# Stationary blocks in chunk order for the first expert pair's one-hot products, and six zero products in the routing's waits

## The reference

```
g_sel  = top-1 of 4 expert groups (x @ w_group);  2 experts e of 8 in that group (x @ w_expert)
h      = silu(x[rows of e] @ w1[e]) * (x[rows of e] @ w3[e])
out   += (h @ w2[e]) * gate        # for each of the 32 experts e
```

## Time and profile before

| what | value |
|---|---|
| time, median of 3 runs | 1101.12 us (1099.44 to 1103.45) |
| the profiled execution: its time | 1100.17 us |
| its span, first to last instruction | 1098.3 us |
| mean granted TensorE clock | 0.992 of full |
| PE busy | 96% of the span |
| DVE, ACT, POOL busy | 37%, 25%, 9% |
| HBM traffic over the span | 266 GB/s; 412 GB/s in the long stretches of the experts |

### The profile page before, as it was taken

How to read it: one execution, slowest core, us unless ns; L and a number is a source line. 1 busy time by engine, 2 the same in 40 slices (tenths; PEclk the granted TensorE clock), 3 DMA queues, 4 the chain that set the end, 5 groups by cost and what they waited for, 6 DMA issues and landing times.

```text
span 1098.3 us, 12899 instructions
## 1 busy us (share of the span) xinstructions
PE 1053.3 (96%) x4563; PEld 543.0 (49%) x4597; DVE 401.2 (37%) x975; ACT 272.8 (25%) x530; POOL 99.7 (9%) x146
## 2 busy tenths in 40 slices
PE   6999999999999999999989999999999999999998
PEld 3577655333333334676655333333334844555543
DVE  1164424443443351462343443344430222333221
ACT  4244322111111003334321111111112005564300
POOL 1220221000000002210121000000000200000000
PEclk9899999999999999999999999999999999999999
DMA  8526227999999996427246999999979537822000
GB/s 299 195 78 256 103 87 246 386 412 411 412 413 412 411 399 208 128 82 302 77 172 228 398 412 413 412 412 412 413 289 389 199 36 201 310 85 77 1 1 38
DMA packets 95326, 280.44 MB, mean 255 GB/s; under 512 B 15957, under 2 KB 29699, under 8 KB 86960
## 3 DMA queue, kind: packets, MB, share of 16 engines
q1 hardware_dynamic: 90208, 273.27, 65.9%
q0 software_dynamic: 5072, 6.56, 1.7%
HBM read 286.98 MB, written 4.72 MB: 266 GB/s over the span
## 4 chain that ended last, share of the span: by engine, by line
PE 75%; SPq 14%; DMA 5%; issue 2%; ACT 2%; DVE 1%; ACTq 0%; DVEq 0%
PE bank L1464 12%; PE bank L922 12%; SPq L583 11%; PE bank L1029 8%; PE bank L954 6%; PE bank L1226 5%; PE bank L1043 5%; PE bank L873 4%; DMA ring<-in_w 3%; SPq L589 3%; PE bank L1610 3%; PE bank L1594 3%; PE bank L1482 3%; PE bank L862 2%; DMA ring<-in_w_in 2%
## 5 line engine op out<-in xcount | busy, mean ns | idle before, releaser
L922 PE MATMUL bank<-ring,arena 128*64 128x512 f32 x1024 | 229.2, 596 | 4.4 <-DMA ring<-in_w 4.4
L1464 PE MATMUL bank<-ring,xfT 128*128 128x512 f32 x320 | 141.5, 596 | 0.0
L922 PEld LDWEIGHTS bank<-ring,arena 128*64 128x64 f32 x1024 | 70.9, 137 | 136.5 <-issue 126.3
L954 PE MATMUL bank<-ring,arena 128*64 128x512 f32 x512 | 116.9, 598 | 0.0
L1029 PE MATMUL bank<-ring,xfT 128*128 128x384 f32 (+2 forms) x256 | 100.1, 544 | 4.8 <-DMA ring<-in_w_in 4.8
L1464 PEld LDWEIGHTS bank<-ring,xfT 128*128 128x128 f32 x320 | 59.3, 190 | 69.3 <-issue 68.3
L873 PE MATMUL bank<-arena 128*128 128x512 bf16 x352 | 86.4, 379 | 1.9 <-issue 0.3
L1632 ACT ACTIVATE arena<-bank 128x512 bf16<-128x512 f32 (+1 forms) x64 | 38.2, 597 | 190.1 <-PE bank L954 190.1
L1969 DVE TENSOR_TENSOR arena<-bank,arena 128x512 f32<-128x512 f32 x60 | 41.5, 691 | 119.4 <-ACT arena L1632 119.4
L1029 PEld LDWEIGHTS bank<-ring,xfT 128*128 128x128 f32 x256 | 49.3, 198 | 45.6 <-issue 26.2
L954 PEld LDWEIGHTS bank<-ring,arena 128*64 128x64 f32 x512 | 33.9, 136 | 68.4 <-issue 68.4
(11 more groups left out here) (379 smaller groups left out, 1132.0 us busy)
## 6 DMA issues: line engine op xcount, KB each, us to landing
ring<-in_w SPq DMA_DIRECT2D x256, 512.0 KB
ring<-in_w SPq DMA_DIRECT2D x64, 1024.0 KB
ring<-in_w_in SPq DMA_DIRECT2D x14, 2048.0 KB
ring<-in_w_in SPq DMA_DIRECT2D x8, 1536.0 KB
ring<-in_w_out SPq DMA_DIRECT2D x6, 2048.0 KB
x_store<-x POOLq DMA_DIRECT2D x4, 512.0 KB, 6.2
ring<-in_w_up_moba SPq DMA_DIRECT2D x1, 2048.0 KB
ring<-in_w_up_sb SPq DMA_DIRECT2D x1, 2048.0 KB
```

Source lines behind the costliest of these rows:

```text
L922: ins = pe.matmul(bank[5][CELL * e:CELL * (e + 1), :], xg[:, par, 4 * h + k, at:at + CELL], view[:, e, :, k, :], start=(h == 0 and k == 0) ...
L954: ins = pe.matmul(bank[5 + n][CELL * e:CELL * (e + 1), :], turned[:, par, c, CELL * e:CELL * (e + 1)], down_view(s)[:, e, c, n * HALF:(n + ...
L1464: ins = pe.matmul(dst[:, :], xfT[:, k, t * P:(t + 1) * P], w[:, k, :], start=(k == 0), stop=(k == KD - 1))
```

## The change

ACT copies both tiles of x into chunk order, in three pieces, among its work after the projection. The copy of tile 0 goes to `x_rows[:, 0, :]`, which is free until the rows of pair 2 are fetched, that of tile 1 to a part of `y_words[:, 0]`, free until the outputs of pair 0. The one-hot products read their stationary blocks from these copies. POOL's zeroing of `x_rows[:, 0, :]` is dropped. PE issues four products with the zero matrix ahead of the wait for `picked`, and two ahead of the wait for `kept_or_exp` and `hots_ready`; they add zero to the accumulators.

```diff
+        x_chunks = [x_rows[:, 0, :].rearrange("p (k i) -> p k i", k=KD),
+                    y_words[:, 0, 0:D].rearrange("p (k i) -> p k i", k=KD)]
...
                 copied(pool, plan, "yTa0", "yTa1")
-                pool.memset(x_rows[:, 0, :], 0.0)
                 pool.memset(y_words[:, 1, :], 0.0)
...
+            def add_zeros(n):
+                for i in range(n):
+                    pe.matmul(bank[i % 4][:, :], zeros[:, 0:P], zeros, start=False, stop=False, skip_group_check=True)
...
                 zero_acc()
+                add_zeros(4)
                 pe.wait_ge(picked, 2 * l + 2)
...
+                add_zeros(2)
                 q0 = l * PAIRS
                 pe.wait_ge(kept_or_exp, 3 * l + 2)
                 pe.wait_ge(hots_ready, 2 * l + 1)
...
-                                            x[:, t, :].rearrange("p (i k) -> p k i", k=KD)[:, 4 * half + k, :],
+                                            x_chunks[t][:, 4 * half + k, :],
...
+                def by_chunk(t, a, b):
+                    act.activation(x_chunks[t][:, :, a // KD:b // KD],
+                                   x[:, t, a:b].rearrange("p (i k) -> p k i", k=KD), ACT.Copy)
+
                 turned_raw(0, 0)
                 turned_raw(0, 1)
                 sum_squares(0, x[:, 0, :], "out0", "out1")
                 sum_squares(1, x[:, 1, 0:HALF], "out2")
+                by_chunk(0, 0, D)
+                by_chunk(1, 0, HALF)
                 turned_raw(1, 0)
                 sum_squares(2, x[:, 1, HALF:], "out3")
                 turned_raw(1, 1)
+                by_chunk(1, HALF, D)
```

## The result

| | before | after |
|---|---|---|
| time, median of 6 runs each | 1099.40 us (1097.04 to 1103.45) | 1094.74 us (1089.01 to 1096.93) |
| ratio of the runs, 95% interval | | 0.9946 [0.9927, 0.9964] |
| span of the profiled execution | 1098.3 us | 1091.8 us |
| mean granted clock of that execution | 0.992 | 0.997 |

The change makes the kernel faster, by 5.9 us by the ratio (0.0054 x 1099.4; the interval is 4.0 to 8.0 us), by 4.7 us between the medians and by 6.5 us between the two profiled executions. The forecast was 1091.2 us in a range of 1089.0 to 1096.5: the time lies inside, 3.5 us above the forecast, and the gain of 9.0 us was too large. It lies nearer to the rival "ACT pays" (1093.3).

What follows compares the result with a forecast made beforehand. PE was taken to be bound by stepped weight loads in the one-hot products; dense blocks gain 9.0 us, while ACT's copies, zero products and the dropped memset count 0: 1100.17 - 9.0 = 1091.2 us, range 1089.0 to 1096.5 us.

Steps and rivals of the forecast that it cites:

- ACT pays: Rival, chance 0.18: ACT's stepped copies slow by factor 2.3, routing 1.07 us late in each layer, 1093.3 us in all.
- The bound: One-hot products of pair 0, both layers, 16.29 us: PE's loads read every eighth word, 335 ns against 192 ns for L1195.
- The products, 9.0 us: One-hot products with blocks in one piece: 4.55 us gained in layer 0, 4.62 in layer 1, less 0.2 us.
- 16 products in 1.78 us: Chain time of L1195's products with neighbouring reads, taken as the new time of each half of the one-hot products.
- ACT, 0.0 us: ACT's copies before the L1817 of 163.28 us: 2.34 us in a 2.30 us gap, taken as no loss.
- the prediction's own signs: Forecast wrong if a half stays near 4 us, ACT's 1024-element copy exceeds 1.6 us, or row or weight waits grow.
- the bounds: ACT's first two copies: nothing lost, or slowed by 2.3 to 3.37 us, 1.07 us more than the gap per layer.
- the estimate of 1.26 ns: ACT's time per stepped element: 0.84 ns plus 0.42 ns from the slow transposes of L862; copies 2.34 us.
- the factor 2.3: One-hot products' slowdown on PE, 4.08/1.78, applied to ACT's stepped copies as the far bound.
- The zero products cost nothing and keep the clock: Six zeros in PE's waits of 1.48 and 0.89 us: no cost, and no clock fall around either layer's one-hot products.
- What was to be late next: Slot products, gate tables and pair 1 rows covered by 0.4, 1.8 and 2.3 us; weight stream starts 4.5 us sooner.
- The sum: Whole kernel: 1100.17 - 9.0 = 1091.2 us against the profiled execution; forecast chance 0.64.

## Why the prediction was right, and where it was off

- **The bound: right.** The one-hot products were slow through the step of their loads. 335 ns fell to 191 ns, as the row of L1195 had said, and the two kernels that differ in this read alone lie 8.2 us apart. (L1195 is not alike in all but the step, as the prediction had it: its blocks have 96 rows and not 128. Its loads take 192 ns all the same.)
- **The products, 9.0 us: too much by 0.6 us.** Measured 4.09 + 4.27 = 8.36 us. The term "16 products in 1.78 us" was mis-sized: a half takes 1.96 us (169.41 to 171.37) and 1.99 us (171.60 to 173.59) up to the start of the line that follows. The pace was right: single records start 112 ns apart in both lines. But 1.78 us is the piece of the chain after the end of the line ahead. The timeline has 1.95 us, and 1.79 us up to the start of the next line:
```profile
103.36 1.95 PE L1195 MATMUL bank<-arena 96*128 96x128 f32 x16
```
L1195 has other products right before and behind it. Each half of L1373 starts behind a wait or another line and ends before one: its second record comes 185 and 214 ns after the first, and the next line 211 and 205 ns after its last record. The prediction took 0.2 us off for such starts in all. Its sum before that, 9.17 us, was 0.8 us too high, about 0.2 us for each half.
- **ACT, 0.0 us: wrong.** It is 0.57 and 0.56 us, and the copy of 1024 elements takes 2.04 us: one of the prediction's own signs that the forecast is wrong (over 1.6 us) came true. The choice between the bounds failed: the row nearest by its step, the slow transposes of L862 (0.42 ns per element more), was PE's and not ACT's, and there the longer loads (195 against 141 ns) cost no time, since the transposes start 112 ns apart (L862) and 109 ns apart (L1308). ACT's element costs 1.78 ns with the step, so the estimate of 1.26 ns was low and the factor 2.3 high (1.93 ns). The rival "ACT pays" had the mechanism and the place right, at 1.07 us per layer about twice the size. Copies with neighbouring reads, and copies on DVE, took the loss away (8.76 us for that stretch).
- **The zero products cost nothing and keep the clock: right** in after, at 166 to 178 and 570 to 578 us. In the ten profiles with these zeros the clock fell shortly before or in the products in 4 of 20 layers, in the two without (before, and the change without zeros) in 4 of 4. Without them 3.2 us of the gain are gone by the times; that the clock is worth nothing under stepped loads and much under dense ones, as the prediction had it, is shown by the pair of kernels without zeros and with zeros alone. It is not safe: with ACT late the clock fell ahead of the zeros in two kernels, and with the zeros alone it fell during the products of layer 1.
- **The clock elsewhere: not foreseen.** The sum let the rest of the kernel keep its clock. It fell at the start of layer 1 in the profiled execution, 1.48 us, and the start of the kernel was 0.89 us faster for the opposite reason (0.91 granted from 20 to 40 us, against 0.83 before). With the wait at the layer's end (0.53 us) this is 1.48 - 0.89 + 0.53 = 1.12 us lost outside the change.
- **Luck in three places.** The first expert product (173.59 us), the gates (176.97) and the rows of pair 1 (181.32) came within 0.1 us of the forecast, but by errors that cancel: the start was 0.89 us early, against 0.57 us of ACT and 0.46 us too much gain from the products of layer 0.
- **What was to be late next: right.** Slot table 170.80 (PE 171.37), gates 176.97 (PE 178.79), rows of pair 1 at 181.32 without a wait, the ring's stream moved with PE: 230.60 against 230.41 us from the first expert product to the last pair. One detail was wrong: the fetch moved by 1.3 us to 174.09 us although the prediction had it fixed by the store of x; 0.89 us of this is the earlier start of the kernel, and it had cover either way.
- **The sum.** 9.0 - 0.64 (products) - 1.13 (ACT) = 7.2 us of the change's own; less 1.12 us elsewhere, and with 0.4 us of small differences in the other stretches, that is the 6.5 us between the profiles. The 5.9 us [4.0, 8.0] of the timed runs hold both and not 9.0.

## What to carry to other kernels

Where the stationary block of an fp32 product is read with a step of 4 words or more, its load takes some 330 ns at either clock, instead of 192 ns at the upper one (in transposes, 195 instead of 141 ns at a step of 8, and no time lost); a copy into one piece pays if an engine with a free gap makes it, and the copy's own step is to be priced on that engine (here DVE, not ACT). Once products are dense, the clock behind a wait becomes worth money: fill the wait with products into an accumulator that stands open or is free, and look at the granted clock of the whole kernel afterwards. A gap of 2.3 us that an estimate fills to within 0.04 us is no cover; one row of the wrong engine is not a price.

## What the runs showed of the hardware

- The price of a step has an edge between 2 and 4 words for fp32: 16 products in 2.02 (neighbouring), 2.15 (2), 3.97 (4) and 4.04 us (8), and ACT's element at 0.81 (neighbouring) and 1.78 ns (8), with 4 and 16 words close to 8.
- DVE makes the stepped copies in about half of ACT's time: 1.10 us for 1024 elements at a step of 8 and 0.62 us for 512, where ACT takes 2.04 and 1.13 us. What the step costs DVE stays open, since no run has this copy of DVE's with neighbouring words.
- ACT pays for a stepped write nearly as for a stepped read (2.86 and 3.07 us for the two copies, 1.56 us without a step).
- Sixteen stepped products take 4.04 us with the clock at 1.00 and 4.10 to 4.17 us with it at 0.50, while dense ones take 2.02 us at 1.00 and 3.75 us at 0.50. At 0.50 a dense product comes every 213 ns and a stepped one every 240, so there the step hardly costs anything.
